# Six modulation vectors summed over the partitions: on POOL instead of TensorE, and another order of DVE's work at one seam

## What is computed

```python
c_act = jax.nn.silu(c)
mod = (c_act @ w_ada[l] + b_ada[l])[:, None, :]
sh1, sc1, gt1, sh2, sc2, gt2 = jnp.split(mod, 6, axis=-1)
h = rms_norm_2(x, g_pre_mix[l]) * (1.0 + sc1) + sh1
z = h @ w_in[l]
...
mix = (g_a * o_a + g_b * o_b) @ w_o[l]
x = x + gt1 * rms_norm_2(mix, g_post_mix[l])
h = rms_norm_2(x, g_pre_ffn[l]) * (1.0 + sc2) + sh2
u = causal_dwconv(h @ w_up[l], conv_w[l], conv_b[l])
y = (jax.nn.silu(u[..., :D_FF]) * u[..., D_FF:]) @ w_down[l]
x = x + gt2 * rms_norm_2(y, g_post_ffn[l])
```

## Time and profile before

| | us |
|---|---|
| median of 3 runs | 1902.23 (1901.94 to 1903.13) |
| the profiled execution, its own time | 1901.29 |
| its span, first to last instruction | 1899.6 |
| PE busy, share of the span | 99% |
| DVE, ACT, POOL busy | 72%, 55%, 5% |
| granted TensorE clock, mean | 1.000 |

### The profile page before, as it was taken

The page is one execution under the profiler, slowest core; times in us unless marked ns, Lnnn a source line. Parts: engine busy times, 40 slices in busy tenths (PEclk is TensorE's granted clock), DMA queues, the critical chain, the costliest instruction groups (busy, mean ns, idle before and its releaser), DMA issues.

```text
span 1899.6 us, 29882 instructions
## 1 busy us (share of the span) xinstructions
PE 1885.5 (99%) x9895; PEld 1600.7 (84%) x9895; DVE 1365.6 (72%) x1889; ACT 1038.8 (55%) x1689; POOL 102.5 (5%) x168
## 2 busy tenths in 40 slices
PE   9999999999999999999999999999999999999998
PEld 7888888888889988888888788888888888888886
DVE  7777777887767556678777877777777766655555
ACT  6545546654545544457654445666566666544444
POOL 3000001000000112211100000000000000000000
PEclk9999999999999999999999999999999999999999
DMA  8888787798777754476678885777777766465553
GB/s 304 288 307 263 247 268 264 267 350 278 265 266 231 233 169 130 136 224 203 216 251 287 302 296 176 233 244 232 232 236 240 232 199 188 160 205 191 195 195 137
DMA packets 233225, 443.52 MB, mean 233 GB/s; under 512 B 14363, under 2 KB 108197, under 8 KB 232000
## 3 DMA queue, kind: packets, MB, share of 16 engines
q1 hardware_dynamic: 229840, 428.27, 68.2%
q0 software_dynamic: 3248, 14.29, 2.4%
q10 hardware_dynamic: 64, 0.02, 0.0%
HBM read 438.28 MB, written 4.24 MB: 233 GB/s over the span
## 4 chain that ended last, share of the span: by engine, by line
PE 97%; DVE 1%; ACT 1%; issue 0%; DMA 0%; ACTq 0%; DVEq 0%
PE PS L2071 57%; PE PS L2561 17%; PE PS L2565 9%; PE PS L2441 3%; PE PS L2451 2%; PE PS L2230 1%; PE PS L2239 1%; PE PS L2126 1%; PE PS L2249 1%; PE PS L2250 1%; PE PS L2247 1%; PE PS L2217 1%; PE PS L2219 1%; PE PS L2135 0%; PE PS L2206 0%
## 5 line engine op out<-in xcount | busy, mean ns | idle before, releaser
L2071 PE MATMUL PS<-w_hi,aT 128*128 128x512 f32 (+1 forms) x3264 | 1045.0, 394 | 1.7 <-DVE w_lo L1280 0.8
L1280 DVE TENSOR_TENSOR w_lo<-raw,w_hi 128x1024 fp32r<-128x1024 f32 (+2 forms) x624 | 754.5, 1213 | 387.2 <-ACT w_hi L730 379.6
L730 ACT ACTIVATE w_hi<-raw 128x1024 fp32r<-128x1024 f32 (+2 forms) x624 | 651.1, 1047 | 568.2 <-PE PS L2071 319.2
L2071 PEld LDWEIGHTS PS<-w_hi,aT 128*128 128x128 f32 x3264 | 611.7, 188 | 132.1 <-issue 5.4
L2071 PE MATMUL PS<-w_lo,aT 128*128 128x512 f32 (+1 forms) x1632 | 633.0, 388 | 0.0
L2561 PE MATMUL PS<-aT,w_hi 128*128 128x512 f32 x1408 | 442.9, 396 | 1.1 <-DVE aT L1449 1.1
L2071 PEld LDWEIGHTS PS<-w_lo,aT 128*128 128x128 f32 x1632 | 307.0, 188 | 58.9 <-issue 0.2
L2565 PEld LDWEIGHTS PS<-aT,w_lo 128*128 128x128 f32 x1408 | 264.5, 188 | 62.5
L2565 PE MATMUL PS<-aT,w_lo 128*128 128x256 f32 x1408 | 276.6, 278 | 0.0
L1338 DVE SCALAR_TENSOR_TENSOR arena<-ada_raw,silu_c,arena 128x1024 f32<-128x1024 f32 x192 | 246.3, 1283 | 28.7 <-DMA ada_raw<-in_w_ada 28.0
L2561 PEld LDWEIGHTS PS<-aT,w_hi 128*128 128x128 f32 x1408 | 214.4, 189 | 1.8 <-issue 1.8
(11 more groups left out here) (271 smaller groups left out, 1389.9 us busy)
## 6 DMA issues: line engine op xcount, KB each, us to landing
raw<-in_w_in SPq DMA_DIRECT2D x248, 512.0 KB, 4.4
ada_raw<-in_w_ada SPq DMA_DIRECT2D x192, 512.0 KB, 4.9
raw<-in_w_up SPq DMA_DIRECT2D x176, 512.0 KB, 3.6
raw<-in_w_down SPq DMA_DIRECT2D x88, 512.0 KB, 4.0
raw<-in_w_out SPq DMA_DIRECT2D x32, 512.0 KB, 5.7
raw<-in_w_o SPq DMA_DIRECT2D x32, 512.0 KB, 6.1
raw<-in_w_uq SPq DMA_DIRECT2D x24, 384.0 KB, 3.7
raw<-in_w_ukv SPq DMA_DIRECT2D x16, 512.0 KB, 5.2
```

The source lines that it names most:

```text
L730: nc.scalar.activation(part_of(w_hi, m, width), part_of(raw, m, width), ACT.Copy).then_inc(hi_ready, 1)
L1280: nc.vector.tensor_tensor(part_of(w_lo, m, width), part_of(raw, m, width), part_of(w_hi, m, width).bitcast(F32), ALU.subtract).then_inc(lo ...
L2071: mm = pe.matmul(dst, l, r, start=first and j == 0, stop=last and j == 2)
```

## The change

1. All seven sums over the partitions go from PE to POOL. `whole` is one POOL instruction (partition_all_reduce) that reads an accumulator of 128 x 2048 and leaves on every partition the sum of all. For the five that are wanted as columns `own_columns` then masks the result so that partition p keeps only column p of each group of 128, and DVE sums along the free axis from SBUF instead of PSUM. GT1 and GT2 are wanted on every partition and are used as they come.
2. `B_MIX`, its DMA and DVE's two additions go; GT1's bias comes as one row into the accumulator, by a small DMA on POOL's queue. ACT's copy of GT2 goes.
3. Eight of the 16 pieces of SH2's second half move from W_O's panels 1 and 2 (six each before, four and none after) to the last four gate panels (two more each), on SP and on DVE. Its sum is read in slot 3 of W_O's panel 2.
4. At the seam DVE does row tile 1's chain ahead of one split and of residual quarters 2 and 3 of tile 0; `mod_columns` isn't in it any more, PE's `ada_reduce` gives way to `keep_busy(24)`, and `keep_busy(10)` becomes `keep_busy(6)`.

Semaphores, loop strides and the deleted helpers are left out:

```diff
+        SUM_SH1, SUM_SC1, SUM_SC2 = [arena[:, at:at + D] for at in (8192, 10240, 12288)]
+        SUM_SH2 = [arena[:, at:at + D] for at in (16384, 14336)]
+        SUM_GT1 = arena[:, 4096:4096 + D]
+        SUM_GT2 = ada_raw[:, :, :].rearrange("p a n -> p (a n)")
...
-        O_PIECES = ((0, 2, 4, 6), (0, 1, 2, 4, 5, 6), (0, 1, 2, 4, 5, 6), ())
+        O_PIECES = ((0, 2, 4, 6), (0, 2, 4, 6), (), ())
 
         def late_piece(p, slot):
 
-            n = sum(len(q) for q in O_PIECES[:p]) + O_PIECES[p].index(slot)
+            n = 8 + sum(len(q) for q in O_PIECES[:p]) + O_PIECES[p].index(slot)
...
+            gt1 = ada_piece(GT1, 16)
+
+            def gt1_and_sh2(i, slot):
+                gt1(i, slot)
+                if slot in (1, 5):
+                    load_ada(i * P + SLOTS * P, SH2 * D + 1024 * (slot // 5))
+
+            panels(4, W_IN2, C_G + D, upto(W_O, 0), gt1_and_sh2, free_ada_done=6)
...
+            def whole(dst, acc):
+
+                nc.gpsimd.partition_all_reduce(dst, acc, P, bass.bass_isa.ReduceOp.add).then_inc(pool_step, 1)
+                pool.wait_ge(pool_step, T.ready(pool_step))
+
+            def own_columns(t):
+
+                t = t.rearrange("p (k n) -> p k n", k=KT)
+                nc.gpsimd.affine_select(out=t, in_=t, compare_op=ALU.is_equal, fill=0.0, base=0,
+                                        pattern=[[0, KT], [1, P]], channel_multiplier=-1).then_inc(ada_whole, 1)
+                pool.wait_ge(ada_whole, T.ready(ada_whole))
...
-            pool.wait_ge(mod_ready, 2)
+            gate_pieces = credits["ada_done"] + 64 + OUT_PIECES
+            pool.wait_ge(ada_done, gate_pieces - 4)
+            pool.wait_ge(rows_T, T_SEAM_2)
+            whole(SUM_SH1, ADA_1[:, 0:D])
+            own_columns(SUM_SH1)
+            pool.wait_ge(ada_done, gate_pieces - 1)
+            whole(SUM_SC1, ADA_1[:, D:2 * D])
+            own_columns(SUM_SC1)
             nc.gpsimd.memset(ADA_SH2[0], 0.0).then_inc(acc_zeroed, 1)
...
+            pool.wait_ge(ada_done, credits["ada_done"] + 64 + 32)
+            whole(SUM_SC2, ADA_SC2)
+            own_columns(SUM_SC2)
...
+            pool.wait_ge(ada_done, credits["ada_done"] + 64 + 32 + 16)
+            whole(SUM_SH2[0], ADA_SH2[0])
+            own_columns(SUM_SH2[0])
...
+            nc.gpsimd.dma_start(ADA_GT1[0:1, :], b_ada_2[:, GT1 * D:(GT1 + 1) * D]).then_inc(gt1_row_landed, 16)
...
-            nc.gpsimd.dma_start(B_MIX, bass.AP(b_ada_2.tensor, GT1 * D, [[0, P], [1, D]])).then_inc(row_landed, 16)
             for s in range(ST):
                 nc.gpsimd.dma_start(X[:, s, :], x1_dram[s * P:(s + 1) * P, :]).then_inc(x_again, 16)
+            pool.wait_ge(ada_done, credits["ada_done"] + 64 + 32 + 16 + 32 + 8)
+            nc.gpsimd.partition_all_reduce(SUM_GT1, ADA_GT1, P, bass.bass_isa.ReduceOp.add).then_inc(gt1_summed, 1)
+            pool.wait_ge(gt1_summed, 1)
             pool.wait_ge(rows_T, T_SEAM_4)
             nc.gpsimd.memset(ADA_GT2, 0.0).then_inc(acc_zeroed, 1)
             pool.wait_ge(acc_zeroed, 6)
             nc.gpsimd.dma_start(ADA_GT2[0:1, :], b_ada_2[:, GT2 * D:(GT2 + 1) * D]).then_inc(ffn_row_landed, 16)
-            pool.wait_ge(rows_ready, 8)
-            nc.gpsimd.dma_start(G_FFN, bass.AP(g_post_ffn_2.tensor, 0, [[0, P], [1, D]])).then_inc(ffn_row_landed, 16)
+            pool.wait_ge(ada_done, credits["ada_done"] + 64 + 96)
+            whole(SUM_SH2[1], ADA_SH2[1])
+            own_columns(SUM_SH2[1])
+            pool.wait_ge(x2_ready, 7)
+            nc.gpsimd.dma_start(G_FFN, bass.AP(g_post_ffn_2.tensor, 0, [[0, P], [1, D]])).then_inc(ffn_gain_landed, 16)
+            pool.wait_ge(ada_done, credits["ada_done"] + 64 + 96 + 32)
+            nc.gpsimd.partition_all_reduce(SUM_GT2, ADA_GT2, P, bass.bass_isa.ReduceOp.add).then_inc(gt2_summed, 1)
...
+            act.wait_ge(ada_cols_read, 3)
...
-                    if last and slot == 6:
-                        act.wait_ge(spread_done, 3)
-                        nc.scalar.activation(ADA_GT2, PS[:, 0:4, :].rearrange("p b n -> p (b n)"), ACT.Copy)\
-                            .then_inc(g_copied, 1)
...
+            def mod_sums(part, src, before=None):
+
+                dve.wait_ge(ada_whole, T.ready(ada_whole))
                 total = tmp_b[:, 0, :]
-                link(nc.vector.tensor_reduce(total, PS[:, bank:bank + 4, :].rearrange("p b (k n) -> p (b k) n", k=4),
-                                             AX.X, ALU.add))
-                nc.vector.tensor_tensor(mod[:, part, :], total, col[:, C_ADA + KT * part:C_ADA + KT * (part + 1)],
-                                        ALU.add).then_inc(mod_ready, 1)
+                nc.vector.tensor_reduce(total, src.rearrange("p (k n) -> p k n", k=KT), AX.X, ALU.add)\
+                    .then_inc(ada_cols_read, 1)
+                dve.wait_ge(ada_cols_read, T.ready(ada_cols_read))
+                if before is None:
+                    before = col[:, C_ADA + KT * part:C_ADA + KT * (part + 1)]
+                nc.vector.tensor_tensor(mod[:, part, :], total, before, ALU.add).then_inc(mod_ready, 1)
...
-            mod_sums(SH1, B_ROT)
+            mod_sums(SH1, SUM_SH1)
...
-                    if j == 9:
-                        mod_sums(SH2, B_UP1)
...
-            panel(0, ("mla", 0), None, qs_out)
+            panel(0, ("mla", 0), None, lambda p: (mod_sums(SH2, SUM_SH2[0]), qs_out(p)))
...
+                        ada(ADA_SH2[1], slot // 5, p + SLOTS)
...
-                if slot in (3, 6):
-                    half = slot // 6
-                    cols = slice(1024 * half, 1024 * (half + 1))
-                    dve.wait_ge(spread_done, half + 1)
-                    dve.wait_ge(row_landed, 32)
-                    nc.vector.tensor_tensor(B_MIX[:, cols], PS[:, B_SPREAD:B_SPREAD + 2, :].rearrange("p b n -> p (b n)"),
-                                            B_MIX[:, cols], ALU.add).then_inc(g_read, 1)
-                    dve.wait_ge(g_read, half + 1)
-                    link(nc.vector.tensor_tensor(G_MIX[:, cols], B_MIX[:, cols], G_MIX[:, cols], ALU.mult))
+                if slot == 6:
+                    dve.wait_ge(row_landed, 16)
+                    dve.wait_ge(gt1_summed, 1)
+                    link(nc.vector.tensor_tensor(G_MIX, SUM_GT1, G_MIX, ALU.mult))
...
+                    if p == 2 and slot == 3:
+                        mod_sums(SH2, SUM_SH2[1], mod[:, SH2, :])
...
             inverse_rms(2, 1)
             diagonal(0, 2)
             residual(0, 1)
-            split()
-            residual(0, 2, 3)
             row_mean(1, 4, 4)
             o_out(3, [1])
             dots(3, [1])
             inverse_rms(1, 1)
             mean_of_sum(1)
             residual(1, 0)
-            mod_columns(SH2)
             inverse_rms(3, 1)
             diagonal(1, 3)
             residual(1, 1)
             split()
             split_unit(0, GROUPS)
             split_unit(1, GROUPS)
+            residual(0, 2)
             residual(1, 2)
             split()
             split_unit(2, GROUPS)
+            split()
+            split_unit(3, GROUPS)
+            residual(0, 3)
             residual(1, 3)
-            split_unit(3, GROUPS)
             split()
...
-            dve.wait_ge(g_copied, 1)
-            link(nc.vector.tensor_tensor(G_FFN, ADA_GT2, G_FFN, ALU.mult))
+            dve.wait_ge(ffn_gain_landed, 16)
+            dve.wait_ge(gt2_summed, 1)
+            link(nc.vector.tensor_tensor(G_FFN, SUM_GT2, G_FFN, ALU.mult))
...
-            pe.wait_ge(ada_done, credits["ada_done"] + 64 + OUT_PIECES)
-            ada_transpose(ADA_1[:, 0:D], B_ROT)
-            for slot in range(SLOTS):
-                chunk(slot, KT)
-            pe.wait_ge(mod_ready, 1)
-            ada_transpose(ADA_1[:, D:2 * D], B_ROT)
-            for slot in range(SLOTS):
-                chunk(slot, KT)
+            for _ in range(2):
+                for slot in range(SLOTS):
+                    chunk(slot, KT)
             for slot in range(SKEW):
...
-                    if (g, kt) == (0, 1):
-                        pe.wait_ge(kr_ready, 1)
-                        pe.wait_ge(ada_done, credits["ada_done"] + 64 + 32)
-                        ada_transpose(ADA_SC2, B_UP1)
...
-                    if first and g == 2:
-                        pe.wait_ge(mod_ready, 4)
-                        pe.wait_ge(ada_done, credits["ada_done"] + 64 + 32 + 16)
-                        ada_transpose(ADA_SH2[0], B_UP1)
...
-                if slot == 2:
-                    columns(EARLY)
-                if slot in (2, 5):
-                    if slot == 2:
-                        pe.wait_ge(ada_done, credits["ada_done"] + 64 + 32 + 16 + 32)
-                    else:
-                        pe.wait_ge(g_read, 1)
-                    spread(ADA_GT1, B_SPREAD, (0, 1) if slot == 2 else (2, 3))
...
-            pe.wait_ge(ada_done, credits["ada_done"] + 64 + 96)
-            pe.wait_ge(acc_free[1], 1 + N_PANELS - 1)
```

(63 more changed lines are left out.)

17 lines of the change are left out of this document (10 added, 7 removed).

## The result

| | us |
|---|---|
| kernel before, median of 4 runs beside it | 1902.33 (1901.94 to 1903.13) |
| changed kernel, median of 4 runs | 1944.29 (1943.44 to 1945.19) |
| ratio | 1.0221, 95% interval 1.0208 to 1.0234 |
| the profiled execution: its time, its span | 1945.19, 1943.5 |
| granted TensorE clock, mean | 0.989 |

What follows compares the result with a forecast made beforehand. PE, busy 99% of the span, was taken to bound the kernel. 13.9 us of PE work removed + 2.1 at the seam - 4.0 given back = 12.0 off 1902.2, so 1890.2 us; range 1885 to 1916.

Steps and rivals of the forecast that it cites:

- Holding DVE up: All seven sums: POOL reading SBUF and DVE's two-input operations exclude each other; each sum with its mask holds DVE 5.7 us.
- 4 us given back: Loss from sums holding DVE: 2 us at SH1 and SC1, about 1 at each of two places in W_O.
- The first rival: At the seven sums, ports are held for the whole sum and stop PE: 1933.8 us; chance 0.27.
- The rival's price: Holds beyond DVE's 5.2 us lead at the seven sums stop PE for 47.6 us in all.
- the pair: SH1 and SC1, summed back to back: 19.8 us of PE stall if ports are held for whole sums.
- The sum: One partition sum of 2048 columns on POOL: 9.3 us, taken as two passes of a two-input operation.
- the window of 15.4: First sum and mask on POOL, from 420.1 to 435.5: 15.4 us available for 12.5.
- the second rival: On POOL, the sum takes far longer than its windows, ports or not: 2904 us at 205 each; chance 0.06.
- PE work removed: Four sets of 16 transposes and the spreads of GT1 and GT2 leave PE's chain: 13.9 us off.
- moved loads: Two more loads and `ada` products in each gate panel are hidden by PE's work: nothing counted.
- The seam: Seam to the up projection: DVE's path starts `row_mean` earlier and PE can follow: 2.1 us off.
- DVE's lead of 5.2 us: How late DVE could start chunk 7's split, from 421.16 to 426.3, before PE waits: 5.2 us.

Runs made afterwards that it cites:

- the run with the code loaded back: The changed kernel with POOL's code for the masked instructions loaded again as POOL's last instruction: 1937.06 us, ratio 1.0187.
- the run with one column: The kernel before with one unread sum over partitions of a single column added at the end of POOL's list: 1909.85 us, ratio 1.0042.

## Why the prediction was wrong

**The step that failed** is in *Holding DVE up*: "I assume that the sum holds the ports only while it reads, at the copy's rate, 2.5 us", and from it "4 us given back". The sum holds them for 9.0 of its 11.9 us, and that costs 52 us. The rows for the opposite were in the prediction (the exclusion of the earlier trace rows is complete for as long as an instruction reads); what carried the assumption was only the thought that a sum over partitions must pass data on for most of its time and needs no port then, and no row showed that. The first rival is what happened. The Trainium skill, SBUF — State Buffer, section "Who interferes with whom", says that the pair of ports is held for the whole instruction, that DVE with two inputs from SBUF contends with what reads on POOL and not with what only writes (a fill), and that DVE with at most one SBUF input outside its two-port modes doesn't contend. The runs agree with the second and the third (a split of 9.68 beside a sum, of 1.22 beside fills; L1887 at 0.69) and nearly with the first: 9.0 of 11.9 us, not the whole.

**The rival's price** was 47.6 us and came to 52.2 by the lag (50.1 by the medians, 1937.06 of the run with the code loaded back less 1886.92 without sums): 19.2 against 19.8 for the pair, 5.1 and 6.0 against 7.3 each, 7.1 against 5, 4.6 against 4.1; only GT1 was far off, 10.2 against 4.1, likely because its sum fell, 10.9 us late through a load of code, on a moment without lead; no run has this sum without the load. That the totals agree is partly luck: 13.4 us of the lag are the lower clock behind the stalls, which the price didn't have, and against that the hold was taken as the whole sum and mask, 12.5 us. With the measured hold and masks (9.0 + 2.4) the rival's rule gives an estimate of some 41 us, and the clock's 13.4 beside it 55.

**What no step had:** the 7.6 us of the start. POOL's code was nowhere in my sum, and the trace of before has no row of it, since there the code is always at hand. The Trainium skill, GPSIMD Engine Reference, section 2.1 "Instruction dispatch", says that the first call of freshly loaded code costs about 6 us that no instruction in the profile shows; by that figure the start would have been an estimated 6 us late. Here POOL stands for 10.3 to 10.4 us (10.27 and 10.38) and the first product comes 7.5 us later.

**Terms by their size.** The sum: 9.3 forecast, 11.9 measured; the mask 3.2, 2.0 to 3.0. Together still inside the window of 15.4: no wait of DVE for POOL is in the list of waits, so the second rival had nothing. It was near: with fills of 13.04 us, and DVE not held up, DVE did wait for POOL (6.7 us). PE work removed, 13.9, and moved loads at nothing: the run without sums has 1886.92 where this gives 1886.2. The seam: 2.1 forecast, 2.2 in the lag; but it isn't the order alone, as I had it by calling the path DVE's: with `ada_reduce` left in PE's list 1.25 us come, and with fewer fillers 2.0. DVE's lead of 5.2 us was read at one place and used at seven.

## What to carry to other kernels

An idle engine isn't free when it reads through ports that a busy engine needs: price such an instruction by its whole length against the other engine's lead at that very place. If the ports let others in between instructions, cut it into pieces, though the sum of them is longer: pieces of 512 columns, shorter than the lead, gave back half of the cost, and pieces of 128 columns all of it at GT2. At the first seam and in W_O, where DVE is busiest, pieces of 128 weren't tried. An instruction of another set of code on POOL is paid for at the next program start as well; look at what the program leaves behind, and load the usual code back where nobody waits. A stall of PE can cost more than its idle time, for the clock behind it is lower: the sums' stalls are 37.8 us of idle time and brought 13.5 us of busy time with them (the run with the code loaded back against the one without sums). The wait at the start brought none (PE busy for 1884.2 us in the run with one column, 1885.5 before).
